# Four tiles of 32 stationary columns in place of 64 + 32 + 32 in the experts' products

## The reference, cut to what matters

```python
def swiglu(h, wg, wu, wd):
    return (jax.nn.silu(h @ wg) * (h @ wu)) @ wd

def step(y, blk):
    tok, wt, e = blk                       # 128 tokens of one expert
    out = swiglu(hf[tok], exp_gate[e], exp_up[e], exp_down[e])
    return y.at[tok].add(out.astype(F32) * wt[:, None]), None
```

## Time and profile before

| | |
|---|---|
| median of 3 runs | 2841.64 us |
| profiled execution | 2839.84 us, span 2837.4 us |
| granted TensorE clock, mean over the span | 0.976 |
| VectorE busy | 1276.7 us (45%) |
| ScalarE busy | 450.3 us (16%) |
| GpSimd busy | 428.2 us (15%) |
| DMA | 433.12 MB, mean 153 GB/s over the span |

### The profile page before, as it was taken

The page is one execution under the profiler, slowest core; times in us unless marked ns, Lnnn a source line. Parts: engine busy times, 40 slices in busy tenths (PEclk is TensorE's granted clock), DMA queues, the critical chain, the costliest instruction groups (busy, mean ns, idle before and its releaser), DMA issues. The chain is left out here.

```text
span 2837.4 us, 30729 instructions
## 1 busy us (share of the span) xinstructions
PE 2664.7 (94%) x11777; PEld 1211.9 (43%) x11778; DVE 1276.7 (45%) x2404; ACT 450.3 (16%) x889; POOL 428.2 (15%) x779
## 2 busy tenths in 40 slices
PE   6998899999999999889999959999999999999995
PEld 3445648778547883446874531111111111111112
DVE  3469636666124336873443483333223333233324
ACT  1024611211001004252320100000000000000001
POOL 0022001210000001000000023222222222222204
PEclk9999999999999999999999879999999999999998
DMA  7411005562403971021031118356555445436617
GB/s 321 200 52 60 1 31 207 210 221 82 155 24 142 404 278 60 15 91 46 3 123 58 52 56 369 141 191 234 204 213 201 157 181 196 162 122 236 279 40 289
DMA packets 71163, 433.12 MB, mean 153 GB/s; under 512 B 16228, under 2 KB 16884, under 8 KB 46994
## 3 DMA queue, kind: packets, MB, share of 16 engines
q0 software_dynamic: 39488, 245.00, 22.7%
q1 hardware_dynamic: 31570, 186.65, 17.1%
HBM read 462.47 MB, written 68.73 MB: 187 GB/s over the span
## 5 line engine op out<-in xcount | busy, mean ns | idle before, releaser
L2872 PE MATMUL psum<-arena 128*32 128x512 f32 x2016 | 1005.3, 612 | 21.2 <-DMA arena<-in_exp_gu,arena 20.3
L2874 PE MATMUL psum<-arena 128*32 x1008 | 527.3, 605 | 0.0
L965 PE MATMUL psum<-arena 128*128 128x256 f32 x1904 | 417.0, 381 | 2.6 <-PEq L1005 1.7
L965 PEld LDWEIGHTS psum<-arena 128*128 128x128 f32 x1904 | 361.6, 191 | 63.3 <-issue 14.6
L2872 PEld LDWEIGHTS psum<-arena 128*32 128x32 f32 x2016 | 165.7, 121 | 452.2 <-issue 451.1
L2947 DVE STREAM_TRANSPOSE arena<-arena 32x256 f32<-32x256 f32 x688 | 299.5, 435 | 18.3 <-DMA arena<-scratch_h,arena 9.4
L2874 PEld LDWEIGHTS psum<-arena 128*32 128x32 f32 x1008 | 69.2, 108 | 409.8 <-issue 409.8
L2958 DVE TENSOR_TENSOR arena<-arena,psum 128x256 f32<-128x256 f32 x42 | 17.7, 422 | 412.2 <-ACT arena L2921 412.2
L2953 DVE COPY arena<-psum 128x512 f32<-128x512 f32 x42 | 29.1, 692 | 300.0 <-PE psum L2874 300.0
L1067 PE MATMUL psum<-arena 128*128 128x512 f32 x352 | 151.8, 592 | 0.3 <-PEq L1091 0.3
L2921 ACT ACTIVATE arena<-psum 128x256 f32<-128x256 f32 x42 | 16.1, 384 | 724.3 <-PE psum L2874 724.3
(11 more groups left out here) (572 smaller groups left out, 2948.8 us busy)
## 6 DMA issues: line engine op xcount, KB each, us to landing
scratch_expert_out<-arena SPq DMA_DIRECT2D x18, 2048.0 KB, 20.5
arena<-in_w_ada SPq DMA_DIRECT2D x12, 2048.0 KB, 17.3
arena<-in_ada_w POOLq DMA_DIRECT2D x12, 2048.0 KB, 8.6
arena<-in_w_up SPq DMA_DIRECT2D x22, 1024.0 KB, 4.9
scratch_expert_out<-arena SPq DMA_DIRECT2D x42, 512.0 KB, 2.7
arena<-in_w_in SPq DMA_DIRECT2D x9, 2048.0 KB, 10.3
arena<-in_w_down SPq DMA_DIRECT2D x5, 2048.0 KB, 8.5
arena<-in_w_o SPq DMA_DIRECT2D x2, 2048.0 KB, 8.3
```

Of the source, the lines that this page charges most:

```text
L965: last = pe.matmul(out, w[:, k, :], x[:, k, :], start=(k == 0), stop=(k == KH - 1))
L2872: pe.matmul(bank[r, :], left[:, r], weights[:, OWN, col:col + 512], start=first, stop=last_)
L2874: return pe.matmul(bank[0:GUEST, :], left[:, 0:GUEST], picked, start=first, stop=last_)
```

## The change

The slots 32 to 127 are taken as three groups of 32 in place of one of 32 and one of 64. The first 32 slots, their weights and the order of the calls (they come last) stay.

```diff
             def rows_of(bank, left, weights, lane_pick, col, first, last_):
-                for r in (slice(GUEST, 2 * GUEST), slice(2 * GUEST, P)):
+                for r in (slice(m, m + GUEST) for m in range(GUEST, P, GUEST)):
                     pe.matmul(bank[r, :], left[:, r], weights[:, OWN, col:col + 512], start=first, stop=last_)
                 picked = weights[:, bass.ds(lane_pick, 1), col:col + 512].rearrange("p a n -> p (a n)")
                 return pe.matmul(bank[0:GUEST, :], left[:, 0:GUEST], picked, start=first, stop=last_)
```

## The result

The changed kernel takes 2322.03 us (median of 4 runs, 2319.95 to 2324.35) against 2841.9 before: a ratio of 0.8169, 95% interval 0.8155 to 0.8183, or 520 us less. The forecast was 2346, the range 2300 to 2430. The profiled run took 2324.35 us, its span is 2322.0.

A forecast was written before the change was run, and what follows sets the result against it. TensorE, busy 94% of the span, was taken as the bound. Gains of 19 (front end), 471 (39 blocks) and 5 us (last down products), 495 in all off 2839.84, gave 2345, adjusted to 2346 us; range 2300 to 2430.

The forecast's parts named there:

- k with four tiles: One of a block's 12 matmul steps, as four 32-column products: 0.89 us, where it had taken 1.98.
- block on TensorE: TensorE's time for one block, 12 steps plus transposes and width changes: 11.25 us, against 25.15 before.
- fourth block starts: Front end: TensorE reaches its fourth block when the weights arrive, at 1757 us instead of 1776.2; gain 19 us.
- 39 blocks: Blocks after the front end: 510 us against 981, each three-block window taking the larger of 33.8 us and DMA time.
- DMA at its full rate: DMA engines when full, as while the first blocks' weights arrive: 408 GB/s.
- Four tiles share the array: In each matmul step, four 32-column tiles run beside each other on TensorE, at most 0.93 us a group.
- The DMA as next bound: Expert weight loads become late next: two-expert blocks need 18 us of DMA against TensorE's 11.25.
- Covers: Other engines stay hidden under TensorE's 11.25 us block: VectorE 8.0 us a block, GpSimd's round of gathers 9.2 us.
- Rival 1: TensorE waits for weights and stays at a slow clock: about 2515 us (2420 to 2690), chance 0.10.
- Rivals 2, 3 and 4: Four-tile groups drain: about 2380 us, chance 0.10; tiles only pair: about 2705, 0.05; shared weight reads serialize: about 3635, 0.02.

The follow-up runs named there:

- the first experiment: Kernel before the change (64 + 32 + 32 columns) with the 64-column tile put first in each step: 2800.24 us, ratio 0.9857.
- the last kernel: Changed kernel with down-weight gathers issued one block later and only half of the gate and up steps: 2284.77 us, ratio 0.8047.

## Why the prediction was right

By its own terms, in the profiled run (forecast 495 us less, measured 2837.4 - 2322.0 = 515.4):

| term | forecast | measured |
|---|---|---|
| k with four tiles | 0.89 us | 0.86 |
| block on TensorE | 11.25 us | 10.8 |
| fourth block starts | 1757 | 1760.38 |
| 39 blocks | 510 us | 2247.60 + 0.37 - 1760.38 = 487.6 |
| DMA at its full rate | 408 GB/s | about 420 |

TensorE was through with its third block at 1754.92 + 0.37 = 1755.3 and then waited 5.02 us for the fourth block's weights. The whole stage began 1707.92 - 1705.50 = 2.4 us later than in the trace before, so from the first matmul to the fourth block it took 52.5 us where 51.5 were forecast.

- *Four tiles share the array:* right, from the row of line 244 alone, and shown by the timeline and the runs with equal cuts. The reading of the earlier trace rows, that the wide tile drains the pair, is shown by the first experiment.
- *The size of the block* was off, by 0.44 us. The trace of the kernel before had shown it, in the next weight loads of line 244, behind the row at 571.68:

```profile
572.14 0.13 PEld L244 LDWEIGHTS psum<-arena 128*32 128x32 f32 x4 [0.30 <-issue]
572.57 0.13 PEld L244 LDWEIGHTS psum<-arena 128*32 128x32 f32 x4 [0.30 <-issue]
```

  The first slot takes 572.14 - 571.68 = 0.46, the second 0.43, and 0.97 is left for the last two, up to the next line at 573.54. So both the start and the end of the 1.86 us held a change of width; I charged one. The lower bound of 0.85 was nearly right.
- *The 39 blocks* hold what was missed: 510 - 487.6 = 22.4 us, against 3.4 the other way at the fourth block's start. It is tempting to put it down to the block, since 39 x 0.44 = 17. But in the forecast's sum the block counts only in the four windows that go by TensorE: 374.6 + 4 x 32.4 = 504, 6 us less. The other 17 us are the nine windows that went by DMA time; the busy share priced them too high.
- *The DMA as next bound:* right in kind, and in size with some luck. The forecast's 510 is 439 of TensorE (39 x 11.25) and 71 of loads. Measured, it is 39 x 10.81 = 421.6 and 66, or 71 with the wait of the fourth block; the run without loads gives 73 over the whole kernel. That the two agree so well has luck in it: the rate was better than 408, and three-block averages missed waits. By bytes at 420 GB/s and 32.4 us for three blocks the larger-of sum is some 472, so about 15 us are not in it; taking the DMA time by share had stood in for them, as the forecast meant it to. The run with the down gathers later took 28 us off, so loads released late are enough to account for them.
- *Covers:* VectorE and GpSimd held. The one wait for VectorE after the change is 3.7 us in the first block.
- *Rival 1 (slow clock):* the mechanism is there, the size is not. After a wait four slots take 2227.97 - 2224.61 = 3.36 us in place of 1.72, close to the 1.73 that the forecast priced; the granted clock over 1707 to 2220 is 0.94, not 0.5. In the run without loads the matmuls took 17.6 us less; that is what the slow slots add to TensorE's work, where the forecast priced 67 for 39 restarts. What they add to the time was not tried by itself: most fall where the DMA is full, and the run with half the steps was faster at a lower clock still, but neither shows that they are free.
- *Rivals 2, 3 and 4* are refuted by 0.86 us a k. Three tiles that read the same weight columns at once cost nothing. The Trainium skill's ratio of 3.07 for four packed row tiles, which the prediction tried on a k (page "TensorE: Matmul & The Clock Gate", Part 3, Measured speedup vs the span model) does not hold for this stream: four tiles take the time of one, 10.8 us a block against 10.5 for the whole product.

## What to carry to other kernels

When a product is cut along its stationary columns, cut it into equal widths: in this kernel the single wider tile ran alone and drained the others at both ends, and the sum of busy times of a line doesn't show it, the starts in order of time do. Before pricing a faster engine, add up per stretch what the next resource needs, and take the larger of the two per stretch of prefetch depth, not over the stage. Once an engine no longer covers the loads, release them in the order in which they are used: that edit was worth nothing before the change and 28 us after it.

## What the runs showed of the hardware that was not expected

Issuing a k as four tiles rather than one whole product costs nothing that shows up in a k (0.86 us either way), though it takes four times the weight loads and a register step for one of them. The DMA held more than its first 50 us had shown (408 GB/s): in the last kernel 403 to 432 GB/s through 29 slices of 13.1 us in a row. Nine tenths of those bytes were gathers from GpSimd's queue (189.84 of 211.45 MB between 1690 and 2215).
